# Branch and output projections of the first block as three fp32r products each, with six blocks of the first branch ahead of the second branch's transposes

## What is computed

```python
xn = rms_norm(h, norm_mix_g)
proj = xn @ w_in                         # all queries, keys, values and gates
o_sb  = stick_breaking_attention(...)    # first branch,  256 x 512
o_gla = gla_chunked(...)                 # second branch, 256 x 512
o_gla = o_gla * rsqrt(mean(o_gla**2) + EPS) * gla_norm_g * silu(g_r)
y = (sigmoid(gate_sb + b_gate[0]) * (o_sb @ w_branch_sb)         # 512 x 1024
     + sigmoid(gate_gla + b_gate[1]) * (o_gla @ w_branch_gla))   # 512 x 1024
h = h + y @ w_out                                                # 1024 x 1024
h = h + conv_ffn(rms_norm(h, norm_ffn_g))
```

## Time and profile before

| | |
|---|---|
| median of 3 runs | 1475.26 us (1472.32 to 1478.39) |
| profiled execution, its time | 1478.23 us |
| profiled execution, its span | 1476.5 us |
| TensorE busy | 1394.1 us, 94% |
| VectorE, ScalarE, GpSimd busy | 676.2, 287.5, 421.9 us |
| HBM read | 479.26 MB, 325 GB/s over the span |
| mean granted clock of TensorE | 0.987 of full |

### The profile page before, as it was taken

How to read it: one execution, slowest core, us unless ns; L and a number is a source line. 1 busy time by engine, 2 the same in 40 slices (tenths; PEclk the granted TensorE clock), 3 DMA queues, 4 the chain that set the end, 5 groups by cost and what they waited for, 6 DMA issues and landing times.

```text
span 1476.5 us, 21029 instructions
## 1 busy us (share of the span) xinstructions
PE 1394.1 (94%) x7640; PEld 785.6 (53%) x7641; DVE 676.2 (46%) x1124; ACT 287.5 (19%) x445; POOL 421.9 (29%) x432
## 2 busy tenths in 40 slices
PE   7999999999989999999999999999999999999995
PEld 6999858999966753433433433433343334334332
DVE  6665336766645453434433444434344444333233
ACT  3645014444424310010100100100010000001001
POOL 4000012322223234344424353434444443200000
PEclk9999999999999999999999999999999999999998
DMA  8544344555535688999996999999999999999994
GB/s 278 173 143 143 114 140 146 192 177 193 167 112 178 238 361 373 427 426 429 429 428 284 427 427 430 427 427 428 426 430 427 427 427 430 427 427 427 430 426 202
DMA packets 77415, 480.76 MB, mean 326 GB/s; under 512 B 7019, under 2 KB 31272, under 8 KB 52808
## 3 DMA queue, kind: packets, MB, share of 16 engines
q1 hardware_dynamic: 74046, 477.45, 79.8%
q10 hardware_dynamic: 3338, 2.88, 0.7%
HBM read 479.26 MB, written 1.05 MB: 325 GB/s over the span
## 4 chain that ended last, share of the span: by engine, by line
PE 50%; DMA 39%; POOL 4%; DVE 2%; issue 1%; ACT 1%; ACTq 1%; POOLq 1%; SPq 0%; DVEq 0%
DMA stage<-in_w_gate_up 25%; PE bank L2230 10%; DMA ring_b<-in_w_gate_up 9%; PE bank L1969 8%; PE bank L1751 6%; PE bank L2306 6%; DMA ring_b<-in_w_down 5%; PE bank L1981 4%; PE bank L1696 4%; POOL ring L616 3%; PE bank L1901 2%; PE bank L1767 2%; PE bank L2211 1%; PE bank L1686 1%; PE bank L2265 1%
## 5 line engine op out<-in xcount | busy, mean ns | idle before, releaser
L616 POOL COPY ring<-stage 128x1024 f32<-128x1024 f32 x300 | 310.9, 1080 | 442.2 <-DMA stage<-in_w_gate_up 358.2
L2230 PE MATMUL bank<-ring,x_T 128*64 128x512 f32 x1584 | 364.7, 605 | 40.2 <-POOL ring L616 32.6
L2230 PEld LDWEIGHTS bank<-ring,x_T 128*64 128x64 f32 x1584 | 110.1, 138 | 272.4 <-issue 202.3
L2306 PE MATMUL bank<-ring_b,act_T 128*64 128x512 f32 x1056 | 238.0, 600 | 1.2 <-ACT act_T L917 0.5
L1566 DVE TENSOR_TENSOR h<-h,bank 128x512 f32<-128x512 f32 x128 | 82.2, 683 | 241.8 <-PE bank L2265 241.8
L2306 PEld LDWEIGHTS bank<-ring_b,act_T 128*64 128x64 f32 x1056 | 72.3, 137 | 149.7 <-issue 127.3
L2230 PE MATMUL bank<-ring_b,x_T 128*64 128x512 f32 x528 | 120.6, 598 | 2.7 <-DMA ring_b<-in_w_gate_up 2.7
L911 ACT ACTIVATE sig<-bias_raw 128x512 f32<-128x512 f32 x33 | 20.8, 629 | 509.0 <-DVE bias_raw L1572 509.0
L1542 DVE SCALAR_TENSOR_TENSOR y_lo<-bank,slot_gate,y_hi 128x512 fp32r<-128x512 f32 x33 | 24.8, 750 | 196.7 <-ACT y_hi L897 196.7
L1969 PE MATMUL bank<-h_hi,ff_hi 128*128 128x256 f32 x352 | 99.8, 284 | 2.2 <-POOL h_lo L548 1.7
L1969 PE MATMUL bank<-h_lo,ff_hi 128*128 128x256 f32 x352 | 99.6, 283 | 0.0
(11 more groups left out here) (445 smaller groups left out, 1791.5 us busy)
## 6 DMA issues: line engine op xcount, KB each, us to landing
stage<-in_w_gate_up SPq DMA_DIRECT2D x75, 2048.0 KB, 25.0
ring_b<-in_w_down SPq DMA_DIRECT2D x64, 2048.0 KB, 23.0
ring_b<-in_w_gate_up SPq DMA_DIRECT2D x32, 2048.0 KB, 21.5
ring<-in_w_gate_up SPq DMA_DIRECT2D x21, 2048.0 KB, 25.5
ring<-in_w_in SPq DMA_DIRECT2D x22, 1024.0 KB, 5.2
ring<-in_w_ffn_in SPq DMA_DIRECT2D x22, 1024.0 KB, 5.1
ring<-in_w_ffn_out SPq DMA_DIRECT2D x11, 1024.0 KB, 4.9
ring<-in_w_out SPq DMA_DIRECT2D x8, 1024.0 KB, 5.5
```

Of the source, the lines that this page charges most:

```text
L616: ins = pool.tensor_copy(pair_slot(g, pair)[:, cols], t.stage[:, pair, cols])
L2230: ins = pe.matmul(banks[n][rows, :], t.x_T[:, c, :], job_slot(g, c)[:, c0:c0 + 512], start=False, stop=(c == GU - 1), skip_group_check=True)
L2306: ins = pe.matmul(banks[4][rows, :], t.act_T[:, k, SLOTS * (c // 2):SLOTS * (c // 2) + SLOTS], job_slot(g, GU + c)[:, c0:c0 + 512], start= ...
```

## The change

All products with chunks 20 to 27 become three fp32r products, so `SPLIT` is 28. The loads, the roundings on ScalarE and the subtractions on VectorE go on through chunk 27 in the ways they had for 0 to 19. The activations get hi and lo parts: `o_sb` and `o_glaT` in two pairs of 512 columns each, `y_T` in eight parts of 256 columns, one for each y. The order on TensorE changes: six blocks of the first branch, the transposes, the last two, then all eight of the second branch. A rounding also waits for the split of the chunk three before. Some buffers are placed anew. (Left out here: semaphores and buffer declarations.)

```diff
-SPLIT = 20
+SPLIT = 28
 # ScalarE
         if n >= HI:
             act.wait_ge(*split_used(g, n - HI))
+            act.wait_ge(s.w_split, n - HI + 1)
         act.activation(t.w_hi[:, n % HI, :], t.ring[:, n % RING, :], ACT.Copy).then_inc(s.w_rounded, 1)
...
+    def o_high(n):
+        pair_of = slice(2 * n, 2 * n + 2)
+        act.wait_ge(*r1.drained(f"o{n}"))
+        act.activation(t.o_hi[:, pair_of, :], t.o_sb[:, pair_of, :], ACT.Copy).then_inc(s.o_rounded, 1)
+    def gla_high(n):            # the same of o_glaT, once ogt{n} is drained
+    def y_turned_high(f):
+        act.wait_ge(s.y_ready, f + 1)
+        act.activation(t.y_hi_T[:, f, :], t.y_T[:, f, :], ACT.Copy).then_inc(s.y_rounded, 1)
     w_hi(19)
-    for n in range(4, 8):
-        gate(n)
+    gate(4)
+    gate(5)
+    w_hi(20)
+    o_high(0)
+    o_high(1)
+    w_hi(21)
+    gate(6)
+    gate(7)
+    w_hi(22)
     for b in range(NB):
         take(r1, f"og{b}", t.o_gla[:, b, :], r1.bank(f"og{b}")[:])
+    w_hi(23)
+    for n in range(2):
+        gla_high(n)
+    for f in range(3):
+        y_turned_high(f)
+    w_hi(24)
+    y_turned_high(3)
+    w_hi(25)
+    for f in range(4, KT):
+        y_turned_high(f)
+    w_hi(26)
+    w_hi(27)
...
-    act.wait_ge(s.y_ready, KT)
     ffn_hi("a", 0, 0)
     ffn_hi("g", 0, 0)
 # VectorE
     sb_out(1)
+    split_lo(20)
+    for n in range(2):          # o_lo = o_sb - o_hi, by pairs, once rounded
+    split_lo(21)
+    split_lo(22)
     dve.wait_ge(*r1.drained("og1"))
...
+    for n in range(2):          # gla_lo = o_glaT - gla_hi, by pairs, once rounded
+    split_lo(23)
+    def y_low(f):
+        dve.wait_ge(s.y_rounded, f + 1)
+        dve.tensor_tensor(t.y_lo_T[:, f, :], t.y_T[:, f, :], t.y_hi_T[:, f, :].bitcast(F32),
+                          ALU.subtract).then_inc(s.y_split, 1)
     for f in range(KT):
...
         dve.tensor_tensor(y_b, bank[:, 1, :], t.gates[:, KT + f, :], ALU.mult).then_inc(done, 1)
+        if f >= 1:
+            y_low(f - 1)
         dve.wait_ge(*r1.drained(f"y{f}"))
         dve.tensor_tensor(t.y_T[:, f, :], y_a, y_b, ALU.add).then_inc(s.y_ready, 1)
+    split_lo(24)
+    y_low(KT - 1)
+    split_lo(25)
     step(dve.memset(t.a_pad[:, 0], 0.0))
     dve.memset(t.a_pad[:, 1], 0.0).then_inc(s.ff_zero, 1)
...
+    split_lo(26)
+    split_lo(27)
     add_mixed(0, 0)
+    add_mixed(0, 1)
     ffn_lo("a", 0, 0)
-    add_mixed(0, 1)
     add_mixed(1, 0)
 # TensorE
+        for part, (wt, xt) in enumerate(((w_hi, x_hi), (w_lo, x_hi), (w_hi, x_lo))):
+            if f == 0 and part != 1:
+                pe.wait_ge(s.o_rounded if part == 0 else s.o_split, 2 * q + 2)
+            if f % 4 == 0 and part < 2:
+                pe.wait_ge(s.w_rounded if part == 0 else s.w_split, n + 1)
+            for k in range(4):
+                ins = pe.matmul(bank[:, q * T:(q + 1) * T], wt[:, k, cols], xt[:, k, :],
+                                start=(part == 0 and k == 0), stop=(part == 2 and k == 3))
         if q == 1:
             ins.then_inc(s.filled, 1)
+        elif f % 4 == 3:
+            ins.then_inc(s.w_used, 1)
-    for f in range(4):
+    for f in range(6):
         branch(f, 0)
     pe.wait_ge(s.o_n_ready, 1)
     for n in range(2):          # the eight transposes of o_n, as before
...
-    branch(4, 0)
-    pe.wait_ge(*r1.drained("ogt1"))
-    for f in range(4):
+    for f in (6, 7):
+        branch(f, 0)
+    for f in range(KT):
         branch(f, 1)
...
+    def mixed_out(col, blocks, n):
+        into = [open_bank(r1, f"wo{col}{b}") for b in blocks]
+        for half, part in ((0, 0), (0, 1), (1, 0), (1, 1), (0, 2), (1, 2)):
+            w_hi, w_lo = split_parts(g, n + half)
+            wt, yt = ((w_hi, t.y_hi_T), (w_hi, t.y_lo_T), (w_lo, t.y_hi_T))[part]
+            if part == 0:
+                pe.wait_ge(s.w_rounded, n + half + 1)
+                pe.wait_ge(s.y_rounded, 4 * half + 4)
+            elif part == 1:
+                pe.wait_ge(s.y_split, 4 * half + 4)
+            else:
+                pe.wait_ge(s.w_split, n + half + 1)
+            for bank, b in zip(into, blocks):
+                for k in range(4):
+                    ins = pe.matmul(bank[:], yt[:, 4 * half + k, b * P:(b + 1) * P], wt[:, k, :], ...)
...
+            if col == 0 and (half, part) == (0, 1):
+                ins.then_inc(s.w_used, 1)
+    mixed_out(0, (0, 1), 24)
+    mixed_out(1, (0,), 26)
     for b in range(NB):
         pe.wait_ge(*r1.drained(f"wo0{b}"))
         turn_quarter(r1, "hT", t.h, b, 0)
-    project(r1, "wo11", 1, wo, t.y_T, 0, 512)
+    mixed_out(1, (1,), 26)
```

More of the change, by code:

```diff
@@ L237, in build @@
         t.persistent(into(ctx))
-        for phase in (t.vectors, t.mixer, t.ffn, t.attention, t.last_out, t.experts):
+        for phase in (t.vectors, t.mixer, t.branches, t.ffn, t.attention, t.last_out, t.experts):
             with ExitStack() as stack:
@@ L759, in scalar_program @@
     act.activation(t.gates[:, 0:KT], t.gates[:, 0:KT], ACT.Sigmoid).then_inc(s.gate_sig, 1)
-    w_hi(19)
-    for n in range(4, 8):
-        gate(n)
+    def o_high(n):
[3 more added lines that the diff above has]
+    def gla_high(n):
+        pair_of = slice(2 * n, 2 * n + 2)
+        act.wait_ge(*r1.drained(f"ogt{n}"))
+        act.activation(t.gla_hi[:, pair_of, :], t.o_glaT[:, pair_of, :], ACT.Copy).then_inc(s.o_rounded, 1)
+    def y_turned_high(f):
+        act.wait_ge(s.y_ready, f + 1)
+        act.activation(t.y_hi_T[:, f, :], t.y_T[:, f, :], ACT.Copy).then_inc(s.y_rounded, 1)
+    w_hi(19)
+    gate(4)
[7 more added lines that the diff above has]
+    w_hi(22)
     for b in range(NB):
         take(r1, f"og{b}", t.o_gla[:, b, :], r1.bank(f"og{b}")[:])
+    w_hi(23)
[10 more added lines that the diff above has]
+    w_hi(27)
     def pad(i, q):
@@ L1186, in vector_program @@
     sb_out(1)
+    split_lo(20)
+    for n in range(2):
+        pair_of = slice(2 * n, 2 * n + 2)
+        dve.wait_ge(s.o_rounded, n + 1)
+        dve.tensor_tensor(t.o_lo[:, pair_of, :], t.o_sb[:, pair_of, :], t.o_hi[:, pair_of, :].bitcast(F32),
+                          ALU.subtract).then_inc(s.o_split, 1)
+    split_lo(21)
+    split_lo(22)
     dve.wait_ge(*r1.drained("og1"))
@@ L1201, in vector_program @@
         dve.tensor_tensor(t.o_glaT[:, pair, :], bank, t.gr[:, pair, :], ALU.mult).then_inc(done, 1)
+    for n in range(2):
+        pair_of = slice(2 * n, 2 * n + 2)
+        dve.wait_ge(s.o_rounded, n + 3)
+        dve.tensor_tensor(t.gla_lo[:, pair_of, :], t.o_glaT[:, pair_of, :], t.gla_hi[:, pair_of, :].bitcast(F32),
+                          ALU.subtract).then_inc(s.o_split, 1)
+    split_lo(23)
[3 more added lines that the diff above has]
+                          ALU.subtract).then_inc(s.y_split, 1)
     for f in range(KT):
@@ L1897, in branch @@
         n = 20 + 2 * (f // 4) + q
-        landed(n)
+        x_hi, x_lo = ((t.o_hi, t.o_lo), (t.gla_hi, t.gla_lo))[q]
+        w_hi, w_lo = split_parts(g, n)
         bank = open_bank(r1, f"y{f}") if q == 0 else r1.bank(f"y{f}")
-        for k in range(4):
-            ins = pe.matmul(bank[:, q * T:(q + 1) * T], chunk(g, n, (4, 512))[:, k, P * (f % 4):P * (f % 4) + P],
-                            (t.o_sb, t.o_glaT)[q][:, k, :], start=(k == 0), stop=(k == 3))
+        cols = slice(P * (f % 4), P * (f % 4) + P)
+        for part, (wt, xt) in enumerate(((w_hi, x_hi), (w_lo, x_hi), (w_hi, x_lo))):
[6 more added lines that the diff above has]
+                                start=(part == 0 and k == 0), stop=(part == 2 and k == 3))
         if q == 1:
             ins.then_inc(s.filled, 1)
-    pe.wait_ge(*r1.drained("o1"))
-    for f in range(4):
+        elif f % 4 == 3:
+            ins.then_inc(s.w_used, 1)
+    for f in range(6):
         branch(f, 0)
@@ L1916, in tensor_program @@
         ins.then_inc(s.filled, 1)
-    branch(4, 0)
-    pe.wait_ge(*r1.drained("ogt1"))
-    for f in range(4):
+    for f in (6, 7):
+        branch(f, 0)
+    for f in range(KT):
         branch(f, 1)
[L1921 to L1933, removed]
+    def mixed_out(col, blocks, n):
[12 more added lines that the diff above has]
+                for k in range(4):
+                    ins = pe.matmul(bank[:], yt[:, 4 * half + k, b * P:(b + 1) * P], wt[:, k, :],
+                                    start=((half, part) == (0, 0) and k == 0), stop=((half, part) == (1, 2) and k == 3),
+                                    skip_group_check=True)
+                if (half, part) == (1, 2):
+                    ins.then_inc(s.filled, 1)
+            if col == 0 and (half, part) == (0, 1):
+                ins.then_inc(s.w_used, 1)
+    mixed_out(0, (0, 1), 24)
+    mixed_out(1, (0,), 26)
     for b in range(NB):
@@ L2437, in __init__ @@
         self.o_n_ready = new("o_n_ready")
+        self.o_rounded = new("o_rounded")
+        self.o_split = new("o_split")
         self.y_ready = new("y_ready")
+        self.y_rounded = new("y_rounded")
+        self.y_split = new("y_split")
```

(17 more changed lines are left out.)

## The result

| | before | after |
|---|---|---|
| median | 1478.39 us (5 runs, 1472.32 to 1480.5) | 1469.5 us (5 runs, 1468.33 to 1469.96) |
| span of the profiled execution | 1476.5 us | 1467.8 us |
| first branch product to the transposes of the last columns of h | 56.94 us | 49.56 us |

The five runs of before include the three of the table ahead. The ratio is 0.9947, 95% interval 0.9924 to 0.9970: faster, by an amount that lies on either side of the 0.5% that a measurement can tell, 0.46% having been forecast. A second comparison gave 0.9961 (0.9945 to 0.9976; 1469.52 us in 11 runs, 1475.38 before in 29). Each ratio is worked out from all runs and is not the quotient of the two medians.

A forecast was written before the change was run, and what follows sets the result against it. TensorE's own products were taken to bound both edited stretches. 10.2 us saved, less stalls of 0.5, 0.25, 0.25 and 2.35, gave 6.85 us, so a median of 1468.5 us from 1475.26, range 1463.5 to 1473.

The forecast's parts named there:

- the two classes: Outcomes for the whole time: over 0.5% faster, given 0.38, and no change that a measurement can tell, given 0.57.
- Products, 10.2 us: Branches and output projection on TensorE: products alone fall from 55.1 to 44.9 us, 10.2 us less.
- Up to 173 us: First branch: nothing moves ahead of 160.25 us; block 6 waits for a bank that VectorE frees, a 0.5 us stall.
- y turns: Second branch, 174.6 to 187.8 us: VectorE turns of 1.48 us; roundings 24 and 25 hold turns by 0.55 and 0.67.
- Column half 0: Output projection, first half: two TensorE stalls of 0.25 us, for the last y's rounding and then its low part.
- Column half 1: Output projection, second half: GpSimd's ff_lo goes between splits 26 and 27, so TensorE stalls 2.35 us.
- the four small operations: Evidence on engine order: four small VectorE operations amid twelve GpSimd copies took 3.68 us, waiting one copy each.
- Rigid tail: Everything behind the output projection moves rigidly with its end, by the same time.
- A: Splits 26 and 27: VectorE keeps its turn or GpSimd asks late, no 2.35 us stall; 9.2 us gained, 1466.1; 22%.
- B: After the 2.35 us stall the clock falls to 1.2 GHz, costing 1.85 us; 5.0 us gained, 1470.3; 20%.
- C: VectorE's y turn takes 1.84 us, the last y comes later; 4.6 us gained, 1470.7; 11%.
- D: Branch products: weight loads not hidden, 0.184 us a product; 5.6 us slower than before, 1480.9; 5%.

The follow-up runs named there:

- held `ff_lo`: Changed kernel with GpSimd's first ff_lo also waiting until split 27 of the weights is done; 1466.3 us, ratio 0.9950 to the kernel before.
- its pieces: Changed kernel with GpSimd's first ff_lo cut into four unchained pieces of 512 columns; 1466.95 us in 1 run, stretch 47.71 us.
- plain branches: Changed kernel with plain fp32 products in the branches, splits 20 to 23 left out, roundings kept; 1472.0 us, ratio 0.9978 to the kernel before.

## Why the prediction was right

The forecast was 1468.5 us, 0.46% less, with 6.85 us in the stretch; measured were 7.38 in the stretch, and 0.53% in the first comparison and 0.39% in the second. The result lies at the edge between the two classes that the prediction gave 0.38 and 0.57. By its steps:

- *Products, 10.2 us.* 192 x 0.1175 = 22.6 (22.8 said), 96 x 0.234 = 22.4 (22.1): 10.1. Right.
- *Up to 173 us.* Nothing ahead of the branches waited for the new roundings and splits; hold ahead of block 6 0.5. Right. The trace of before said that five blocks would hide both (VectorE ends o_n at 166.8, five blocks would go to 167.4), which I did not draw from it.
- *y turns.* 1.46 us against 1.48, with the two holds by roundings 24 and 25 (0.34 and 0.56 in brackets, for 0.55 and 0.67), last y 27.3 us after the first product against 27.55. Right.
- *Column half 0.* Two stalls of 0.25 were forecast; 0.12 and 0.11 were seen. Twice too large, and small.
- *Column half 1.* The step that carries the rest. The order (split 26, `ff_lo`, split 27) came out as argued from the four small operations among twelve copies, and the gap lies four products before the end of wo10. Its size was 1.8 for 2.35: split 27 ended 42.0 us after the first product instead of 42.65 (a last y 0.26 earlier, a `ff_lo` that ended 0.26 sooner behind it, and 2.16 instead of 2.3 us from there to the end of split 27), and TensorE came to it 0.15 earlier. The margin was thinner than the 0.4 us of the prediction: GpSimd asked 0.23 us before split 26 ended, and 0.09 before the record of split 27 starts. The held `ff_lo` shows the cause, its pieces and the plain branches the rule behind it. The Trainium skill ("SBUF — State Buffer", "Who interferes with whom": two SBUF inputs on VectorE against a GpSimd instruction that reads SBUF, by issue order) has the rule. The traces agree with it in all of these: 6.70, 5.73 and 5.50 us for VectorE subtractions of 2.29, and 6.18 for an `ff_lo` of 4.6 when VectorE was first.
- *Rigid tail.* FFN start to the end is 1250.7, 1250.7, 1250.7 us in three profiles of before and 1247.7 to 1251.2 in nine others, so rigid within 3 us. That is as much as half of what the change brings, and why a time measures it so poorly.
- *Rivals.* A did not occur here, and did in the kernel with plain branches. B did not occur: the clock stayed at 1.00 through the gap (all windows of 190 to 208 us, here and in the three other profiles with the gap). But the gap was shorter than the 2.35 us that B was priced for, so B at that length was not tested. C did not occur, with turns of 1.46 us, nor did D, with 0.1175 us a product.
- *The sum.* The measured terms give 10.1 - 0.5 - 0.12 - 0.11 - 1.8 = 7.57 for 7.38 measured; the 0.2 between them is assigned to nothing.

In the profiled span both misses go the same way, 1467.8 for the 1469.7 forecast: the stretch gave 0.53 more, and the 1.4 us ahead of the branches were not foreseen. The median came out 1.0 above its forecast all the same, 1469.5 for 1468.5. That last step leaned on the median of three runs of before, which was 1475.26, then 1478.39 in five and 1475.38 in 29. The mechanism and the sum for the stretch were right; that the time was met to 1 us, with the span missed by 1.9 the other way, is luck.

## What to carry to other kernels

When work moves from TensorE to VectorE, look on GpSimd's queue for what will now run at the same time: one 4.5 us GpSimd instruction in front of a 2.3 us VectorE one cost 1.8 of the 9.2 us on offer, and a wait, or four pieces, gave them back. What the held instruction meets next must be looked at too: here it held another VectorE split, which nobody needed soon. Whether two such instructions collide hangs on tenths of a microsecond, so it should be put in order by a semaphore and not left to the schedule. A change of 0.5% is read from a profile of its stretch (the same kernel repeated to 0.02 us here, while products that no edit touched differed by up to 0.25 us between variants), not from medians that move by 3 us.

## What the runs showed of the hardware that I had not expected

An idle of TensorE of one length can cost clock in one run and not in the next. At the FFN's last products the idle before them was 2.31 to 2.32 us in every profile. Chain of waits, the changed kernel and the one with held `ff_lo`, with the group before for scale:

```profile
389.97 5.47 PE bank L2067 x24
...
403.50 7.34 PE bank L2067 x24
```

```profile
388.60 5.47 PE bank L2068 x24
...
402.13 5.72 PE bank L2068 x24
```

Windows inside these two groups, in the form of the earlier trace rows; the clock is the third number from the end:

```profile
404.00:405.00 1.00, 1.00 (x4) 0.70 (x4) 0.00 (x0) 0.00 (x0) 0.00 (x0) 0.50 0.88 350
```

```profile
405.00:406.00 1.00, 1.00 (x6) 0.84 (x5) 0.00 (x0) 0.00 (x0) 0.00 (x0) 1.00 0.00 0
```

The group took 7.34 us at a granted clock that fell to 0.50 (1.2 GHz) in one, and 5.72 at 1.00 in the other. The profiles of the two kernels with held `ff_lo` kept 1.6 us by it; in the ten other profiles the clock fell (7.2 to 7.4 us). The gap of the changed kernel, 1.63 to 1.65 us in four profiles, cost no clock in any.

The stretch from the first pooled output product to the first expert product took 53.17, 51.48 and 53.20 us in three profiles of one and the same kernel, before, and 51.5 in all others; in the first of these the clock was 0.59 and 0.55 from 474 to 478 us, in the second 1.00. So the instance that B was argued from usually repeats, but not always: the idle's length alone does not decide, and what does was not shown here.
